# Down-projection weights with two successive rows a partition, and hidden activations turned with every second unit as a column

## What is computed

```python
def expert_block(args):
    xblk, e = args
    hid = jax.nn.silu(xblk @ w_gate[e]) * (xblk @ w_up[e])   # 1024 -> 512 hidden units
    return hid @ w_down[e]                                    # 512 -> 1024
```

## Time and profile before

| | |
|---|---|
| runs, us | 1715.44, 1716.42, 1754.85 |
| median, us | 1716.42 |
| profiled execution, us | 1716.88 |
| its span (first to last instruction), us | 1715.0 |
| TensorE busy | 96% of the span |
| share of the last-ended chain that is TensorE's | 86% |
| mean granted TensorE clock | 0.992 of full speed |
| DMA: packets, MB, GB/s over the span | 109553, 475.29, 277 |
| DMA share in the 1/40 slices of the expert steps | 9 tenths or more, 395 to 409 GB/s |

### The profile page before, as it was taken

How to read it: one execution, slowest core, us unless ns; L and a number is a source line. 1 busy time by engine, 2 the same in 40 slices (tenths; PEclk the granted TensorE clock), 3 DMA queues, 4 the chain that set the end, 5 groups by cost and what they waited for, 6 DMA issues and landing times.

```text
span 1715.0 us, 24253 instructions
## 1 busy us (share of the span) xinstructions
PE 1654.8 (96%) x10112; PEld 1088.4 (63%) x10119; DVE 743.6 (43%) x1281; ACT 327.6 (19%) x545; POOL 76.7 (4%) x76
## 2 busy tenths in 40 slices
PE   8999998999999999989999999999999999999998
PEld 6876686555555555547787787878655555555554
DVE  4899744333333333244453444445433333333333
ACT  4134621101001010123221222222100100000002
POOL 0030001000000000000000000000100000000000
PEclk9999999999999999999999999999999999999999
DMA  8212138999999999994222122127699999999995
GB/s 299 99 56 92 58 147 332 400 401 403 395 409 406 399 402 406 408 367 148 71 77 98 50 99 99 53 99 313 230 395 404 407 406 409 409 402 400 401 404 238
DMA packets 109553, 475.29 MB, mean 277 GB/s; under 512 B 10752, under 2 KB 23040, under 8 KB 76544
## 3 DMA queue, kind: packets, MB, share of 16 engines
q1 hardware_dynamic: 101120, 455.11, 67.7%
q0 software_dynamic: 5248, 8.40, 1.7%
q10 hardware_dynamic: 3072, 10.18, 1.5%
HBM read 476.27 MB, written 6.29 MB: 281 GB/s over the span
## 4 chain that ended last, share of the span: by engine, by line
PE 86%; DVE 8%; DMA 2%; issue 2%; ACT 1%; SPq 1%; DVEq 0%; POOLq 0%; ACTq 0%
PE psum L927 25%; PE psum L951 12%; PE psum L842 9%; PE psum L843 9%; PE psum L844 9%; PE psum L1038 8%; DVE h L2083 2%; PE psum L918 2%; PE psum L1336 2%; DVE xs L1747 2%; PE psum L936 2%; DMA raw<-in_odd_w_in 1%; PE psum L942 1%; DVE w_lo L666 1%; PE psum L1226 1%
## 5 line engine op out<-in xcount | busy, mean ns | idle before, releaser
L2083 DVE TENSOR_TENSOR h<-h,psum 128x512 f32<-128x512 f32 x240 | 154.2, 684 | 246.4 <-PE psum L1038 245.1
L666 DVE TENSOR_TENSOR w_lo<-raw,w_hi 128x2048 fp32r<-128x2048 f32 x46 | 105.4, 2291 | 202.1 <-ACT w_hi L660 202.1
L951 PE MATMUL psum<-raw,hidT 128*64 128x512 f32 x672 | 154.2, 601 | 1.1 <-ACT hidT L1541 1.1
L660 ACT ACTIVATE w_hi<-raw 128x2048 fp32r<-128x2048 f32 x46 | 88.1, 1914 | 335.9 <-PE psum L844 334.9
L842 PE MATMUL psum<-w_hi,uT_hi 128*128 128x512 f32 x352 | 139.5, 396 | 3.4 <-DVE h L2203 1.4
L1559 ACT ACTIVATE y_hi<-psum,rt 128x512 fp32r<-128x512 f32 x62 | 42.6, 687 | 506.9 <-PE psum L1038 366.5
L844 PE MATMUL psum<-w_lo,uT_hi 128*128 128x512 f32 x352 | 137.8, 392 | 0.0
L843 PE MATMUL psum<-w_hi,uT_lo 128*128 128x512 f32 x352 | 137.8, 391 | 0.0
L1038 PE MATMUL psum<-y_hi,to_token 64*128 64x512 f32 (+1 forms) x464 | 107.2, 444 | 20.6 <-DVE h L2083 17.8
L2321 POOL DMA_INDIRECT x_e<-xs_dram,index x64 | 60.3, 942 | 1464.5 <-PE psum L918 785.6
L2062 DVE SCALAR_TENSOR_TENSOR y_lo<-psum,rt,y_hi 128x512 fp32r<-128x512 f32 x66 | 49.2, 748 | 135.1 <-ACT y_hi L1559 135.0
(11 more groups left out here) (257 smaller groups left out, 2505.7 us busy)
## 6 DMA issues: line engine op xcount, KB each, us to landing
raw<-in_expert_w_down SPq DMA_DIRECT2D x84, 1024.0 KB, 23.7
raw<-in_expert_w_up SPq DMA_DIRECT2D x44, 1024.0 KB
free_a<-in_expert_w_gate SPq DMA_DIRECT2D x44, 1024.0 KB
in_pair<-in_expert_w_up SPq DMA_DIRECT2D x42, 1024.0 KB
in_uT<-in_expert_w_up SPq DMA_DIRECT2D x42, 1024.0 KB
free_b<-in_expert_w_gate SPq DMA_DIRECT2D x40, 1024.0 KB, 23.1
in_pair<-in_expert_w_down SPq DMA_DIRECT2D x40, 1024.0 KB, 23.2
xs<-in_expert_w_gate SPq DMA_DIRECT2D x40, 1024.0 KB, 23.7
```

Source lines behind the costliest of these rows:

```text
L660: nc.scalar.activation(part(w_hi[half]), half_of(n, half, by_columns), ACT.Copy).then_inc(hi_ok[half], 1)
L666: nc.vector.tensor_tensor(part(w_lo[half]), half_of(n, half, by_columns), part(w_hi[half]).bitcast(F32), ALU.subtract).then_inc(lo_ok[half ...
L951: mm = nc.tensor.matmul(psum[c * FIRST:(c + 1) * FIRST, bank], x[:, j % 2, (j // 2) * FIRST:(j // 2 + 1) * FIRST], w[:, j, c * 512:(c + 1) ...
L2083: ins = V.tensor_tensor(dst, dst, psum[:, SUM_BANKS[half]], ALU.add)
```

## The change

The DRAM view of the down weights is cut otherwise: a partition p now takes rows 2p and 2p+1 of the first 256 rows, and rows 256+2p and 256+2p+1 of the second 256, so that each 1 MB transfer has one run of 8 KB a partition instead of two of 4 KB. The bytes, the buffers, the number of transfers and their semaphores are the same. Since block j of the weights now holds every second row, `transpose_hidden` picks every second column of `hid` (a step of 2 elements, 8 bytes) for each 128 x 128 piece.

```diff
-        wd_dram = expert_w_down.rearrange("l e (j p) n -> l e p j n", j=HC)
+        wd_dram = expert_w_down.rearrange("l e (h p j) n -> l e p h (j n)", h=2, j=2)
...
                         if kind == "down":
-                            c = slice(half * HC // 2, (half + 1) * HC // 2)
-                            dst, part_of = chunks_of(w, HC)[:, c], one(source[kind], layer, at)[:, c]
+                            dst, part_of = chunks_of(w, 2)[:, half], one(source[kind], layer, at)[:, half]
...
             def transpose_hidden(m, wide):
 
                 for j in range(HC if wide else HC // 2):
-                    mm = nc.tensor.transpose(psum[:, 4, j * P:(j + 1) * P], hid[:, j * P:(j + 1) * P], ident)
+                    at = j // 2 * 2 * P
+                    mm = nc.tensor.transpose(psum[:, 4, j * P:(j + 1) * P], hid[:, at + j % 2:at + 2 * P:2], ident)
```

More of the change, by code:

```diff
@@ L612, in one @@
             taken = src[layer, bass.ds(e, 1)]
-            return taken.rearrange("a p n -> p (a n)" if len(taken.shape) == 3 else "a p j n -> p (a j) n")
+            return taken.rearrange("a p n -> p (a n)" if len(taken.shape) == 3 else "a p h n -> p (a h) n")
         def copied(eng, *name):
@@ L795, in experts @@
                             for k, src in enumerate((wg_dram, wu_dram, wd_dram)):
-                                dst = over_w[k] if k < 2 else chunks_of(over_w[k], HC)
+                                dst = over_w[k] if k < 2 else chunks_of(over_w[k], 2)
                                 sp.dma_start(dst, one(src, layer, e)).then_inc(over_landed[layer], 16)
```

## The result

The change makes the kernel slower by 0.4%. Its median is 1724.24 us (1718.32 to 1727.28 in 11 runs) against 1716.41 for the kernel before; the ratio is 1.0044, with a 95% interval of 1.0033 to 1.0055. The forecast was 1715.6, slightly faster, with a range up to 1721.0. So the time lies above the range, and it moved the other way. Two of the 11 runs before fell into a slower state of the chip (about 1755 us), none of the changed kernel's did; the ratio leaves them out. The profiled execution took 1726.99 us (1716.88 before).

The account below looks back on a forecast made before the run. The prediction took TensorE to set the pace of the expert steps. From 1716.88 us it took 0.9 at the layer boundary and added 0 for the strided load: 1716.0, or 1715.6 as a median, range 1712.5 to 1721.

Parts of the forecast that it names:

- What bounds the kernel: Expert steps: TensorE sets the pace, at 14.66 and 14.44 us a step; the full DMA engines do not.
- The rival that weights pace the steps: Expert steps: unseen waits for weights, so saved transfer time all comes back, giving 1708, at most 1701; chance 0.03.
- Half of the packets gone: Down transfers: 16384 of 109553 packets go; about 4 us of transfer time a layer, hidden except between the layers.
- The boundary: End of layer 0: ACT's 0.94 us wait for the next mixer's first weight block goes; gain 0.9 us.
- The strided load: Weight load in the turning of hid: bounded by 0 and 3.5 us in all, taken as 0.
- this rival: Turning of hid: first load of each pair costs up to 55 ns more, giving 1719.1; chance 0.14.
- The mark for being wrong: Expert steps: the prediction is wrong if steps get longer or shorter by more than 0.1 us each.
- The gathers: Gathers in the steps: 0.6 us later, inside 2.4 us to spare; as rival, 3.5 us longer gives 1751, chance 0.03.
- The sum: Whole kernel: 1716.88 - 0.9 + 0 = 1716.0 against the profiled execution, 1715.6 for a median.

Follow-up runs that it names:

- e1: The changed kernel with its 8 KB transfers, but hid turned in contiguous columns as before; 1719.55 us, ratio to before 1.0011.
- e3: The changed kernel with 8 KB transfers, but DVE writes hid with units side by side and TensorE's load is contiguous; 1718.25 us, ratio 1.0006.
- e4: As e3, but layer 0's down block of expert 1 fetched in 4 KB runs, its hid written plainly; 1715.64 us, ratio 0.9990.
- e2: The kernel before with its 4 KB transfers, but hid turned with a step of 2 columns; 1720.22 us, ratio 1.0020.
- e7: As e3, but SP holds layer 0's blocks from expert 1's down block on until the token store has landed; 1716.57 us, ratio 0.9999.
- e9: The kernel before, with only layer 0's down block of expert 1 in 8 KB runs and its hid turned with step 2; 1719.96 us, ratio 1.0020.
- e5: The kernel before, with hid turned at steps of 1, 2, 3 and 4 columns in successive expert steps; ran once, 1718.62 us.
- e8: The changed kernel run again, unaltered, on the same chip as e6 and e7; 1724.98 us in 6 runs, ratio 1.0041.
- e6: The changed kernel, but layer 0's down block of expert 1 fetched in 4 KB runs and turned in contiguous columns; 1720.35 us, ratio 1.0019.

## Why the prediction was wrong, step by step

Two steps failed. The term for the strided weight load was taken as 0 and measured 4.2 us. The delay of the store of the tokens, 3.2 us, had no term in the sum.

**What bounds the kernel: right.** TensorE sets the pace of the steps; with faster transfers a pair of steps still takes 29.10 us (e1, e3, e4). The rival that weights pace the steps is refuted.

**Half of the packets gone: right in number, and hidden, as said.** The spare time at the end of layer 1 grew. In 2 us windows the transfers fade to 25 GB/s at 1694 to 1696 us before and at 1696 to 1698 now, while the last down product starts at 1695.30 before and at 1705.55 now. Counted from layer 1's first down product, the transfers end about 4 us earlier (458 against 454, in windows of 2 us), near the 4 us a layer that I had taken.

**The boundary: right.** ACT's wait of 0.94 us is gone in every 8 KB kernel and there at 0.91 in e2. "Between" is 0.7 to 0.9 us shorter than before in the 8 KB kernels where the clock in 1190 to 1240 us is the same (0.97). The clean cases are e1, e4 and e7, where layer 0's experts take as long as before: the mixer's first block lands 462.3 to 463.0 us after the first down product instead of 465.7, 2.7 to 3.3 us sooner. Slower steps hide the wait without faster transfers: in e9 (4 KB but for one block, layer 0 at 461.62 us) it is 0.17 us, and in e5 (4 KB) it is gone.

**The strided load: the term that was mis-sized.** I bounded it by 0 and 3.5 us and took 0, since 8 bytes seemed nearer to contiguous than 32. It measured 4.2 us, above the upper bound, because a step of 2 (204 ns) costs a little more than one of 8 (196). The part of the argument on what is exposed fits: 64 ns more on a load and 65 ns on a step, one bare load of the two. The two marks that I had set for this rival, 196 ns and 0.43 us, were met, with 204 and 0.44. The mark for being wrong, more than 0.1 us a step, was too coarse: 64 steps times 0.1 us are 6.4 us, more than the range had above the forecast. The error was to place the unknown between two rows by distance, when nothing in the trace said that the cost grows with distance. The sentence of the Trainium skill ("SBUF — State Buffer", the note on cachelines) by which a second access in a line of 16 bytes keeps full rate would have given 0. For TensorE's weight loads of float32 the runs say otherwise: 205 ns at 8 bytes, 200 at 12, 196 at 16.

**The gathers: the right mechanism at the wrong transfer.** I asked what 8 KB packets do to the other queues and looked only at the gathers in the steps. Those were safe, as worked out: landing at 7.1 us in the median and 8.6 at most, as against 6.9 and 8.6, and no wait in the steps. I didn't ask it of the store of the tokens, the one other large transfer that runs beside a down block. It had landed 0.4 us before DVE's list was ready (268.74 and 269.15), and its delay can be estimated from the trace of the kernel before. At 259 us about 400 of its 512 packets of 4 KB were still to go. The two queues moved 3.34 MB in 8 us, 0.42 MB/us. In pairs of 4 and 4 KB that is 51 pairs a us, 7.8 us for 400; in pairs of 4 and 8 KB 34 a us, 11.8 us. That makes an estimate of 4 us for the delay. 3.0 us were measured; the weight queue's packets are not all of 8 KB (2.15 MB in 293), and the pairs went at 37 a us. Less the 0.4 us to spare the gather comes 2.6 us later; its own 0.3 us more (8.00 against 7.73) and 0.3 us at the lower clock make up the 3.2 us of the profiled execution. This term is missing from the sum altogether.

**The clock.** I treated the clock as given. A longer wait ahead of the first step kept it down for longer, 8 us at half rate instead of 4, but most of the 4 us more passed in the wait, and the stretch from the gather's landing to the first down product got only 0.3 us longer (0.4 in e8 against e6). No run held the clock fixed. What decides how deep the dips around the wide steps are in an execution stays open, and so does whether the change makes them deeper. They differ in kernels that are alike there (0.91 in e3, 0.96 in e1 and e4), and up to 2.5 us hang on one of them.

**The sum.** 1716.4 + 4.2 (loads) + 3.2 (store) - 0.8 (boundary) = 1723.0. The last 1 to 2 us up to 1724.2 and 1725.0 are not accounted for. The mean clock is lower (0.9903 against 0.9918 to 0.9922), which fits deeper dips around the wide steps, but more than half of that difference is, by the profiled execution, the longer stretch ahead of the steps (0.0012), whose cost is already in the 3.2. The range failed for a second reason: above the forecast it took in one cost alone, that of the strided load, and two came together.

## What to carry to other kernels

When a transfer's packets grow, look for every other queue that is busy beside it and work out its new share by packets, not by bytes. The one that matters is the transfer that had only just been in time. Both stepped reads measured here cost time, so put such a read on the engine that waits: here 200 ns on DVE were free and 64 ns on TensorE were not. And don't price an unseen stride by the nearest one seen: take the dearest, with room above it, for here 3.5 us from the dearest still fell short of 4.2.

## What was unexpected in the hardware

- A weight load of 128 columns of float32 takes 140 ns when contiguous and 196 to 205 ns at the steps seen (2, 3, 4 and 8 elements); the step's size hardly matters.
- Two hardware queues that are both busy get equal numbers of packets, 424 against 422 in 8 us, even where most of one queue's are twice the size (293 against 293).
- DVE's product of 128 x 256 takes 422 ns, and 622 ns with a step of 2 elements on both inputs and a stepped order of its output.
- Alone on the queue, 2.1 MB in 256 packets of 8 KB is no faster than in 512 of 4 KB; with the queue full the rate rises by 1.5% (401 and 407 GB/s).
